# A streaming encoder trunk on eight cores: engine orders by a list scheduler at build time, blocks of 1152 and 976 columns

## What is computed

```
h  = rmsnorm(x, g_pre_mix)
z  = h @ w_in                                   # 2048 columns: v | gb | gc | u
pooled = multiscale_pool(v)                     # trailing means over 2, 4, 8, 16 frames, minus v
ya = einsum(pooled, pool_mix) * pool_scale      # 4 groups of 128
yb = gb * causal_dwconv(gc * u, conv_w)         # 3 taps in time
mix = concat(head_rmsnorm(ya, 4), head_rmsnorm(yb, 8)) @ w_out
x  = x + rmsnorm(mix, g_post_mix)
h  = rmsnorm(x, g_pre_ffn)
up = causal_dwconv(h @ w_up, ffn_conv_w)        # 2 * 2816 columns, 3 taps in time
x  = x + rmsnorm((silu(up[:2816]) * up[2816:]) @ w_down, g_post_ffn)
```

## Time and profile before

| | us |
|---|---|
| median of 3 runs | 3328.3 (3327.22 to 3330.45) |
| span of the profiled execution, slowest of 8 cores | 3339.3 |
| the same, fastest core | 3298.5 |
| PE busy | 2746.9 (82% of the span) |
| DVE busy | 1872.7 (56%) |
| ACT busy | 1536.5 (46%) |
| POOL busy | 1054.5 (32%) |

### The profile page before, as it was taken

The page is one execution under the profiler, slowest core; times in us unless marked ns, Lnnn a source line. Parts: engine busy times, 40 slices in busy tenths (PEclk is TensorE's granted clock), DMA queues, the critical chain, the costliest instruction groups (busy, mean ns, idle before and its releaser), DMA issues.

```text
span 3339.3 us, 45754 instructions; the slowest of 8 cores (3298.5 to 3339.3 us)
## 1 busy us (share of the span) xinstructions
PE 2746.9 (82%) x13920; PEld 1233.7 (37%) x13920; DVE 1872.7 (56%) x2552; ACT 1536.5 (46%) x3325; POOL 1054.5 (32%) x1080
## 2 busy tenths in 40 slices
PE   1979976997979976996669996878978699787988
PEld 0334432443334432443324443334433344333443
DVE  1567435763567435763556744567535676356763
ACT  1644345442644345443554434644336444265443
POOL 1444124330444124330342312523115332144330
PEclk9989988998989988998889998989989899898999
DMA  9354275445354265437443316243253433534321
GB/s 177 69 93 76 46 119 90 70 70 91 72 93 77 45 118 99 74 66 152 96 77 60 62 36 120 46 86 62 48 100 61 82 64 54 89 68 79 63 45 62
DMA packets 203855, 263.77 MB, mean 79 GB/s; under 512 B 147040, under 2 KB 148832, under 8 KB 203616
## 3 DMA queue, kind: packets, MB, share of 16 engines
q0 software_dynamic: 52992, 189.82, 33.7%
q1 hardware_dynamic: 150624, 71.03, 9.5%
HBM read 406.70 MB, written 9.29 MB: 125 GB/s over the span
## 4 chain that ended last, share of the span: by engine, by line
PE 56%; DMA 13%; DVE 11%; issue 10%; ACT 5%; POOL 3%; SPq 1%; DVEq 0%; ACTq 0%; POOLq 0%
PE psum_all L366 56%; DMA sb_h<-sb_hs 10%; DVE sb_r L400 7%; ACT sb_r L384 4%; POOL sb_x L389 2%; DVE sb_r L389 2%; DVE sb_tp L400 2%; DMA yp<-sb_x 1%; ACT sb_tp L384 1%; DVE sb_hs L400 1%; DMA sb_vec<-vecs 1%; POOL sb_r L389 1%; SPq L510 1%; DVEq L150 0%; ACT sb_cf L404 0%
## 5 line engine op out<-in xcount | busy, mean ns | idle before, releaser
L366 PE MATMUL psum_all<-sb_h,sb_w 128*128 128x512 bf16 (+1 forms) x9600 | 1818.7, 348 | 337.9 <-DMA sb_h<-sb_hs 252.6
L366 PEld LDWEIGHTS psum_all<-sb_h,sb_w 128*128 128x128 bf16 x9600 | 814.6, 99 | 1294.4 <-issue 451.6
L400 DVE SCALAR_TENSOR_TENSOR sb_r<-psum_all,sb_vec,sb_r 128x1023 f32<-128x1023 f32 (+5 forms) x1152 | 1016.0, 886 | 426.6 <-ACT sb_cf L404 295.8
L389 POOL TENSOR_TENSOR sb_r<-sb_r 128x1088 bf16<-128x1088 f32 (+13 forms) x400 | 623.6, 1559 | 1368.6 <-ACT sb_r L384 793.3
L366 PE MATMUL psum_all<-sb_w,sb_r 128*128 128x512 bf16 (+1 forms) x4080 | 891.4, 380 | 16.4 <-POOL sb_r L389 9.1
L384 ACT ACTIVATE sb_r<-psum_all,sb_vec 128x1024 f32<-128x1024 f32 (+2 forms) x736 | 532.3, 759 | 383.2 <-PE psum_all L366 383.1
L384 ACT ACTIVATE sb_r<-sb_r 128x512 f32<-128x512 f32 (+6 forms) x440 | 328.8, 747 | 563.4 <-DVE sb_r L389 527.4
L366 PEld LDWEIGHTS psum_all<-sb_w,sb_r 128*128 128x128 bf16 (+1 forms) x4080 | 399.8, 99 | 499.9 <-issue 33.5
L400 DVE SCALAR_TENSOR_TENSOR sb_tp<-psum_all,sb_ss,sb_g 128x1024 f32<-128x1024 f32 x136 | 174.3, 1282 | 427.8 <-ACT sb_ss L384 373.0
L414 POOL DMA_DIRECT2D sb_w<-wts x360 | 203.4, 567 | 553.9 <-PE psum_all L366 472.9
L400 DVE SCALAR_TENSOR_TENSOR sb_r<-sb_r,sb_vec 128x512 f32<-128x512 f32 (+3 forms) x320 | 227.3, 717 | 251.4 <-ACT sb_r L384 242.8
(11 more groups left out here) (40 smaller groups left out, 572.8 us busy)
## 6 DMA issues: line engine op xcount, KB each, us to landing
sb_w<-wts POOLq DMA_DIRECT2D x360, 512.0 KB, 6.3
sb_g<-gains SPq DMA_DIRECT2D x33, 512.0 KB, 7.0
sb_x<-xp SPq DMA_DIRECT2D x16, 512.0 KB, 5.1
yp<-sb_x SPq DMA_DIRECT2D x16, 512.0 KB, 2.7
sb_h<-sb_hs SPq DMA_TRANSPOSE x136, 3.1
sb_pm<-pm POOLq DMA_DIRECT2D x8, 128.0 KB, 16.6
sb_tp<-gains SPq DMA_DIRECT2D x1, 512.0 KB, 6.2
sb_vec<-vecs SPq DMA_DIRECT2D x1, 312.0 KB, 25.4
```

The lines of the kernel that those rows point to most:

```text
L366: P.op(PE, lambda h: h.matmul(oa, la, ra, start=start, stop=stop), reads=[lv.r(llo, lhi), rv.r(rlo, rhi)], writes=[ov.r(olo, ohi)])
L389: P.op(eng, lambda h: h.tensor_tensor(oa, aa, ba, op), reads=[av.r(alo, ahi), bv.r(blo, bhi)], writes=[ov.r(olo, ohi)])
L400: P.op(DVE, lambda h: h.scalar_tensor_tensor(oa, aa, sc, ba, op0, op1), reads=reads, writes=[ov.r(olo, ohi)])
```

## The change

The engines' orders are no longer the written one. The program's operations are collected with a cost each, and `schedule()` walks a simulated clock at build time and gives each engine, out of the first `LOOK` waiting items, the one that can start first. The eight matmuls of an accumulation go as one item, and so do the four that one tile has with one unit of `w_out` or `w_down`. A weight load (kind "w") is held back in that simulation until the load before the last is nearly in; on the chip this is only a place in POOL's order. The semaphores are then derived as before.

The blocks are cut anew: the first has 1152 prompt frames (9 tiles), the second 896 prompt frames, a gap of 16 columns, and the 64 sample frames, 976 columns in all. z goes by chunks (3 of 384, or 512 and 464), all four groups of a chunk before the next chunk. The sample is part of the last chunk, so it has no matmuls of its own. In u each matmul has two more columns in front (386 or 512 and 466), so that the convolution reads its edge from PSUM, and edge fix-ups fall away; the second block's first two halo columns come from a copy of `h` kept from the first. The d stage does its last two tiles (`NLAST`) together, unit by unit, and each unit is released as it is done; the last tile of o releases its units one by one too. PSUM's eight banks go round in one ring. At the start, only the first three tiles of `h` are prepared before z begins, and the rest of the loads stand behind the first step. The state outputs are stored before the last d stage.

```diff
+NLAST = 2
...
+H0 = 32
+NB0 = 1152
+PR1 = 896
+S1 = 912
+NB1 = 976
...
+        queue = {e: [it for it in items if it.eng == e] for e in ENGINES}
...
+        while left:
+            for e in stale:
+                best, b_start = None, 0.0
+                for it in queue[e][:self.LOOK[e]]:
+                    if it.need:
+                        continue
+                    s = max(free[e], it.ready)
+                    if it.kind == "w" and len(recent) >= 2:
+                        s = max(s, recent[-2] - 1.5)
+                    c = it.cost
+                    if e == ACT and it.kind in ("silu", "root") and it.kind != table:
+                        c += 1.4
+                    if best is None or s + (0.02 if e == PE else 0.5 * c) < b_start:
+                        best, b_start = it, s
+                cand[e] = (best, b_start)
+            stale = set()
+            e = min((x for x in ENGINES if cand[x][0] is not None), key=lambda x: cand[x][1])
+            it, s = cand[e]
+            queue[e].remove(it)
+            streams[e] += it.ops
+            left -= 1
+            stale.add(e)
+            if it.ops[0].is_dma:
+                free[e] = s + (0.62 if e == POOL else 0.15)
+                k = it.kind
+                if k == "w":
+                    b = max(s + 1.6, link["w"])
+                    link["w"] = b + 3.2
+                    done = b + 4.2
+                    recent.append(done)
+                    stale.add(POOL)
+                elif k == "t":
+                    b = max(s + 1.0, link["t"])
+                    dur = 2.6 if link["w"] > b else 1.5
+                    link["t"] = b + dur
+                    done = b + dur + 0.9
+                else:
+                    b = max(s + 1.4, link["d"])
+                    dur = it.cost * (1.7 if link["w"] > b else 1.0)
+                    link["d"] = b + dur
+                    done = b + dur + 1.2
...
+        ring = [0]
+
+        def take_banks(n, even=False):
+            if even and ring[0] % 2:
+                ring[0] += 1
+            s = ring[0]
+            ring[0] += n
+            return [(s + i) % 8 for i in range(n)]
...
+                for ci in range(len(chunks)):
+                    for j in range(4):
+                        z_part(j, ci, i)
+                        i += 1
+                        if not started:
+                            started = True
+                            first_loads()
...
+                def tile_mm(ts_, lhs, nk, units, relq=None):
+                    pks = [take_banks(2, True)[0] // 2 for _ in ts_]
+                    for ui in range(nk // 2):
+                        ws, q = units[ui]
+                        for t, pk in zip(ts_, pks):
+                            a, p = t["a"], t["p"]
+                            P.begin()
+                            for kt in (2 * ui, 2 * ui + 1):
+                                for hf in range(2):
+                                    c0_ = (kt % 2) * D + hf * 512
+                                    mm((banks[2 * pk + hf], 0, 512), (lhs[kt], a, a + p), (ws, c0_, c0_ + 512),
+                                       kt == 0, kt == nk - 1)
+                            P.end()
+                        if relq:
                             release(q)
...
+                ubound = [(0, 384), (384, 768), (768, 1152)] if bi == 0 else [(0, 510), (510, NB1)]
...
                 def u_full(i, ws):
                     fs = []
                     for t_ in range(2):
                         jt = i + NPAIR * t_
-                        fv = fa[fa_ctr[0] % 4]
-                        fa_ctr[0] += 1
-                        pk = mm_pair()
-                        for hf in range(2):
-                            u_mm(i, ws, t_, banks[2 * pk + hf], 0, 512 * hf, 512)
-                        conv_ew(fv, 0, 1024, bankpair[pk], 0, jt, p_edge(jt), (b_cf, (l * 44 + jt) * 2))
-                        fs.append(fv)
-                    if has_s:
-                        u_sample(i, ws, fs[0], fs[1])
-                    gate(i, fs[0], fs[1], 0, 1088 if has_s else 1024, POOL)
...
+                        f = (fctr[0] % 4) * NB0
+                        fctr[0] += 1
+                        if bi == 0:
+                            ks = take_banks(3)
+                            for ci, k in enumerate(ks):
+                                u_mm(ws, t_, banks[k], 0, ubound[ci][0] - 2, 386)
...
+                            ks = take_banks(2, True)
+                            base = ks[0] * PBANK
+                            u_mm(ws, t_, banks[ks[0]], 0, -2, 512)
+                            u_mm(ws, t_, banks[ks[1]], 0, 510, NB1 - 510)
+                            conv(f, [(0, 1, NB1, base)], jt, base + S1, base + PR1 - 78)
...
+                lead = [next_unit("u") for _ in range(NLEAD)]
+                for ci in range(len(ubound)):
+                    for i in range(NLEAD):
+                        u_lead(i, lead[i][0], ci)
+                        if ci == len(ubound) - 1:
+                            release(lead[i][1])
                 load_gain("pre", (4 * (l + 1) + G_PREM) if not last_layer else G_FIN)
-                for i in range(NLEAD):
-                    u_half(i, lead[i][0], 1)
-                    release(lead[i][1])
-                    issue_weights()
                 for i in range(NLEAD, NPAIR):
                     ws, wq = next_unit("u")
                     u_full(i, ws)
                     release(wq)
-                    issue_weights()
...
+                waiting = []
+                groups = [[t] for t in tiles[:-NLAST]] + [tiles[-NLAST:]]
+                for gi, grp in enumerate(groups):
+                    pks = tile_mm(grp, actv, NPAIR, du, gi == len(groups) - 1)
+                    for t, pk in zip(grp, pks):
+                        post_tile(t, pk, DVE, ntmp=1 if boundary else 2)
```

929 lines of the change are left out of this document (464 added, 465 removed).

## The result

The changed kernel takes 3044.7 us in the median, the kernel before 3328.8 us on the same chip; the ratio is 0.9128 (95% interval 0.9108 to 0.9149). I had written 2913 with a range of 2800 to 3015. The direction and the larger part hold, 284 us of 415, and 30 us are missing to the range's end. In two of the five executions of the changed kernel one or both dies ran at a granted clock of 0.83 to 0.89 and took 3372 and 3396 us, so in what follows only runs are compared in which no die ran at a lower clock; of `e3_both` there is no such run, and its undisturbed cores 0 to 3 are read.

A forecast was written before the change was run, and what follows sets the result against it. PE was taken to bound the kernel, with 2691 us of work and 648 us of waits and slow clock. The terms took the 3339.3 us span to 2924; less 11, the forecast was 2913, range 2800 to 3015.

The forecast's parts named there:

- between the blocks: Two PE holes between first and second block, 43 us in all: 20 us expected to go, -23.
- From o to u: PE's wait between w_out and u: 7 and 11 us left a layer in first and second block, -72 and -54.
- From d to z: Six seams after w_down: earlier loads let the transpose land near +3.4, PE waiting 4 us instead of 23, -114.
- Work: PE's matmuls over four layers, with 0.1626 us for 384 columns and 0.1634 for 386: 2655.6 us, -35.
- The second block's u: Without the sample's own matmuls and edge work, PE bounds each unit at 6.6 us: -52.
- z and o: Smaller PE waits in these stages fall from 9.9 and 18 us a layer to 6.5 each: -14 and -46.
- Start: Time before z's first matmul: fewer weight loads ahead of the transposes, z starting near 67 us, -5.
- B: Rival: transposes wait for the whole load burst, DVE standing from +9 to +22 at six seams; 3000 us, chance 0.18.
- C: Rival: static orders the chip doesn't keep, z and o losing 18 us in every layer; 3005 us, chance 0.14.
- D: Rival: waits all but vanish, o to u 2 us, seams 0, z and o 2; 2797 us, chance 0.15.
- E: Rival: the busier PE's clock falls to 1.2 GHz for part of the span; a quarter slow gives 3577 us, chance 0.03.
- F: Rival: the change does not act, loads still in a burst because POOL reaches them late; counted as part of B.

The follow-up runs named there:

- e3_both: Changed kernel with o's four weight loads held until the last transpose landed, and ACT's squares in w_out given their own scratch; cores 0 to 3 took 2950 to 2970 us.
- e4_burst: Changed kernel with the last two tiles of w_down one after the other (`NLAST = 1`) in both blocks; 3010 to 3030 us, ratio 0.9052.
- e5_paced_before: Kernel before, with only w_down's last two tiles done together and a weight load released after each unit of them; ratio 0.9956.
- e7_last_by_block: Changed kernel with o's loads held behind the last transpose and w_down's last two tiles together in the second block alone; 2945 and 2946 us.
- e6_alternate_add: Changed kernel with o's loads held behind the last transpose and every second addition of o, and the last, on DVE; 2939 to 2952 us.
- e8_all: Changed kernel with o's loads held, every second addition and the last on DVE, and w_down's final pair in the second block alone; 2912 to 2920 us.

## Why the prediction was off, step by step

**The balance.** The profiled span is 3041.1 us, my sum 2924, so 117 are to be found. By stages the span is 63.3 (start) + 2655.6 (my work) + 67 lost in z + 233 in o and u + 9 in d + 13 behind the last matmul. Against my terms: o and u 233 instead of 72, +161; z with its seams and the way between the blocks 67 instead of 24 + 20 + 52 = 96 (the 52 held o's small waits too), -29; the start 63.3 instead of 70, -7; d +9. The last -18 are in time that I left standing: the stages and holes that I listed for the kernel before make 3308 of its 3339, and of the 31 left over only 13 are there now.

**From o to u: the step that failed.** I wrote that the four loads are the same, "only 2.6 us earlier". They leave from 2 us before o's end (second block) or 1 us after it (first), where they left 11.4 and 11.7 us after: the scheduler gave POOL three of them ahead of its last additions, and I did not read POOL's order there. From that follow both errors. The transposes of the third and fourth tile then take turns with the loads, so u's first chunk, which I had counted as 10.3 us of cover, is itself what waits. And DVE's next copy waits 10.7 us for its buffer, which delays all tiles behind it. Shown: with the loads held behind the last transpose the loss falls from 233 to 140 us; the time falls by 70, since z lost 18 more in that schedule. The picture behind the step was wrong too. I read from the earlier trace rows that a transpose stands in line behind the loads issued up to 3 us after it, and wrote that the trace disagrees with the page on queue rows. The packets of the same trace agree with it. What I had missed is that a transpose consists of many small packets, so that taking turns is slow for it and passes nothing.

The second half of the step is that the last transpose "leaves 15.6 us after o's end": in the first block, layer 1, it leaves at 598.1, 26.5 us after o's end at 571.6, with the loads held no sooner (26.1). That is the pace of two tiles in 10 us against 3.5 us a tile on PE, and u's first convolutions that stand ahead of the last tile on ACT and DVE; how much is whose was not separated. With every second addition on DVE it leaves 21.4 us after o's end, and 32 us more are gained in o and u. What is left then, 108 us, is near what I had for o and u (72, and a part of the small waits).

**From d to z: the size right, the reason wrong.** I took 19 us off at each of six seams because the loads leave earlier and the transpose that counts then lands at +3.4. It landed at +12.7 (issued 448.0, landing 23.4 us, d's end 458.7). Of the eight loads of 442.2 to 454.3, three had landed by then, the fourth landed with it, and the last came 12.1 us later, at 483.5. So it waited neither for a fixed few nor for all of them; 23.4 us is what the 66 turns come to. DVE came to its copy at +8.7, as I had it, and waited 4.1 us. The seams closed all the same, and in the first block they close without any pacing (`e4_burst`). Pacing alone in the old order leaves 13.6 to 18 us of them (`e5_paced_before`). What closes them is in the order: the copy is made behind its own tile, so that one more transpose is ahead of the loads, and all four groups of z's first chunk come ahead of the second, so that stuck transposes are needed later. Both edits in the old kernel bring 107 us; my term was 114. I had both in my text, as a description. I took for the cause what carried a name in the change.

**Pacing costs.** In the first block z lost 11 to 16 us a seam with the pair and 2 without, with the loads of o held (`e7_last_by_block`) or not (`e4_burst`). That it is because two tiles that end together have their sums behind d's end, and z's work on ACT and DVE behind those, is read from the order and not shown by a run. In the second block the pair also makes d 2.2 us longer a layer. There four matmuls with 64 rows alternate with four of 128, and the 240 matmuls with 64 rows are busy 60.8 us against 53.3 where that tile is alone (`e4_burst`), 1.9 us a layer.

**Work** (-35): right. 0.163 us for 386 columns; full clock in dense stretches. **The second block's u** (-52): right, 6.6 to 6.7 us a unit. **z and o** (-14, -46) and **between the blocks** (-23): together with the seams 29 us better than I had. **Start** (-5): 63.3 instead of 70.

**The rivals.** B had the transpose at +22 and I at +3.4; it came at +12.7, so both were wrong on what it waits for, and B on its price of 13 us a seam. C, small waits in z and o from a static order, did not come in z; the order did cost, but at one place, POOL's between o and u. D's seams came true and the rest did not. E: in the runs compared here the granted clock is 1.00 where PE is dense, 0.965 over the span. F did not occur, and by `e4_burst` a burst would have cost nothing on the whole.

**The last wait before u's last chunk.** Some 6 us are lost there in every layer of the changed kernel, also with the loads held, and I had put them down to the last transpose: in the first block PE goes on 2.6 us after it is issued (600.72 after 598.11). Count and order say otherwise. The first three units are 48 matmuls a chunk in the first block. PE's and DVE's timelines, layer 1 (16 + 32 matmuls of the first chunk stand before the first row):

```profile
586.66 8.00 PE L499 MATMUL psum_all<-sb_h,sb_w 128*128 128x386 bf16 x48 [1.78 <-DVE sb_r L547]
600.72 3.70 PE L499 MATMUL psum_all<-sb_h,sb_w 128*128 128x386 bf16 x11 [6.06 <-DVE sb_r L547]
```

```profile
596.70 1.27 DVE L547 SCALAR_TENSOR_TENSOR sb_hs<-sb_x,sb_ss,sb_g 128x1024 bf16<-128x1024 f32 x1
597.89 3.82 DVE L547 SCALAR_TENSOR_TENSOR sb_r<-psum_all,sb_vec,sb_r 128x384 f32<-128x384 f32 x6
```

PE stands after 96 matmuls. The 97th is not the third chunk's first but the fourth unit's, which the scheduler put eight places ahead of it; it waits for DVE, ACT and a weight load, and for no transpose. The first matmul of the third chunk, eight later, is the one that waits for the transposes, and PE does not stand in front of it. In the second block it is the same with the last chunk of 468 columns, which has no idle time before it in the whole run:

```profile
L499 PE MATMUL psum_all<-sb_h,sb_w 128*128 128x468 bf16 x192 | 41.2, 378 | 0.0
```

What PE waits for is a free bank of PSUM. DVE frees it with the fourth of the convolution's operations of 597.89, done near 600.4, and these stand in DVE's order behind the last tile's copy of 596.70. The same copy lets the last transpose go, which is why both come 2.6 us apart each time. So the profile names the right engine. Little would be gained with the bank alone, though: by the times PE would then stand for the last transpose, which lands at 601.2, and come to the third chunk some 2 us sooner (an estimate; it comes there at 603.2). Both hang on the last tile's late copy, and that is what `e6_alternate_add` moved.

**What stays open.** Of the 108 us that `e6_alternate_add` still loses in o and u I have separated no parts; the profile puts waits of 3.1 us in the first block and of 6.6 to 7.4 in the second to ACT. In this kernel's second block the matmul that stands is the last chunk's first, and by the times it may be the last transpose: in layer 1 it is issued at 2048.5 and lands in 2.7 us, and PE goes on at 2051.6. What sets the pace of two tiles in 10 us was not found. With three loads leaving at o's end the transposes take 10.1 and 10.6 us in the first block's layer 1 and 16.3 and 17.7 in the second's, where their own packets are slow for some 4 us after most of the loads' packets are through (2095 to 2099); why is not known. Why the second block's seams lose 1 to 3 us in one schedule and 9 in another was seen (a wait for DVE of 7.1 us in `e8_all`, for a transpose in `e4_burst`) but not controlled. The way between the blocks went from 15 to over 20 us in the faster kernels and was not tried.
